# A transformer layer on one core: attention's inverse sums as diagonal matrices in the turning products, the second tile turned by halves, the last output pieces signalled singly

## The reference, cut to what matters

```python
def dsa_attention(q, k, v, qi, ki, wi, k_sel):       # 8 heads of 64, queries in 2 blocks of 128
    ...
        logits = jnp.einsum('bqhd,bqkhd->bhqk', qb, ks) * (HEAD_DIM ** -0.5)
        logits = jnp.where(ok[:, None], logits, -jnp.inf)
        p = jax.nn.softmax(logits, axis=-1)
        return jnp.einsum('bhqk,bqkhd->bqhd', p, vs)

def peer_ffn(h, peer_wq, sub_keys1, sub_keys2, peer_u, peer_v):
    q = (h @ peer_wq).reshape(B, T, PEER_HEADS, PEER_QDIM)
    q1, q2 = q[..., :PEER_HALF], q[..., PEER_HALF:]
    s1 = jnp.einsum('bthd,nd->bthn', q1, sub_keys1)
    s2 = jnp.einsum('bthd,nd->bthn', q2, sub_keys2)
    ...                                               # top 16 of each, top 16 of the sums, softmax: gates
    a = gelu(einsum('td,tkd->tk', h, peer_u[eid]));  out = einsum('tk,tkd->td', gate * a, peer_v[eid])

h = h + concat([attention, pooling]) @ w_out
h = h + peer_ffn(rms_norm(h), ...)
return h[:, N_META:]
```

## Time and profile before

| what | value |
|---|---|
| runs | 988.92, 990.38, 988.08 us; median 988.92 |
| span of the profiled execution | 986.2 us, granted TensorE clock 1.000 |
| PE busy | 965.7 us (98%), 6472 records |
| DVE, ACT, POOL busy | 683.2, 465.5, 192.2 us |
| 2 costliest PE lines | L1796 369.3 us, L1444 321.5 us and 64.3 us |

### The profile page before, as it was taken

How to read it: one execution, slowest core, us unless ns; L and a number is a source line. 1 busy time by engine, 2 the same in 40 slices (tenths; PEclk the granted TensorE clock), 3 DMA queues, 4 the chain that set the end, 5 groups by cost and what they waited for, 6 DMA issues and landing times.

```text
span 986.2 us, 18565 instructions
## 1 busy us (share of the span) xinstructions
PE 965.7 (98%) x6472; PEld 885.2 (90%) x6472; DVE 683.2 (69%) x1275; ACT 465.5 (47%) x718; POOL 192.2 (19%) x234
## 2 busy tenths in 40 slices
PE   7999999899999999999999999999999999999998
PEld 7998899888999788999999999999999999999997
DVE  5899758898988786656666565666656565666655
ACT  5566545533777434444344444434344444434442
POOL 3064227986877000000000000000000000000000
PEclk9999999999999999999999999999999999999999
DMA  8634139745212676454555555455555545455554
GB/s 245 187 124 131 46 90 335 190 116 149 79 55 84 217 240 222 172 207 175 194 189 184 199 174 207 172 198 185 185 198 176 207 171 202 180 191 192 178 205 149
DMA packets 70164, 172.57 MB, mean 175 GB/s; under 512 B 6752, under 2 KB 35552, under 8 KB 69616
## 3 DMA queue, kind: packets, MB, share of 16 engines
q1 hardware_dynamic: 68080, 167.47, 50.0%
q0 software_dynamic: 576, 4.19, 2.1%
q10 hardware_dynamic: 1472, 0.44, 0.2%
HBM read 163.16 MB, written 4.72 MB: 170 GB/s over the span
## 4 chain that ended last, share of the span: by engine, by line
PE 74%; DVE 1%; issue 0%; ACT 0%; DVEq 0%; POOL 0%
PE psum L1796 35%; PE psum L1444 31%; PE psum L1754 6%; PE psum L1761 2%; PE psum L1685 1%; DVE big L1111 0%; DVE rr L1207 0%; DVE big L1237 0%; ACT rr L754 0%; ACT big L705 0%; DVE big L1122 0%; PE psum L1742 0%; DVEq L102 0%; ACT raw L700 0%; ACT rr L739 0%
## 5 line engine op out<-in xcount | busy, mean ns | idle before, releaser
L1796 PE MATMUL psum<-rr 128*128 128x512 f32 x1536 | 369.3, 391 | 1.1 <-issue 0.7
L1796 PEld LDWEIGHTS psum<-rr 128*128 128x128 f32 x1536 | 280.7, 188 | 56.2 <-issue 0.9
L1444 PEld LDWEIGHTS psum<-h_all,rr 128*128 128x128 f32 x2592 | 318.8, 188 | 8.3
L1444 PE MATMUL psum<-h_all,rr 128*128 128x256 f32 x2592 | 321.5, 280 | 0.0
L1177 DVE TENSOR_TENSOR rr<-raw,rr 128x1024 fp32r<-128x1024 f32 x109 | 133.5, 1225 | 216.4 <-ACT rr L748 216.4
L748 ACT ACTIVATE rr<-raw 128x1024 fp32r<-128x1024 f32 x109 | 115.6, 1061 | 293.6 <-PE psum L1796 293.6
L633 ACT ACTIVATE rr<-raw 128x1024 fp32r<-128x1024 f32 x107 | 113.6, 1061 | 48.1 <-DMA raw<-in_peer_u_dram 48.1
L1116 DVE TENSOR_TENSOR rr<-raw,rr 128x1024 fp32r<-128x1024 f32 x108 | 131.7, 1219 | 0.5 <-ACT rr L633 0.2
L1163 DVE TENSOR_TENSOR rr<-psum,picks 128x2048 fp32r<-128x2048 f32 x32 | 72.4, 2288 | 9.4 <-PE psum L1754 7.7
L1444 PE MATMUL psum<-rr,h_all 128*128 128x256 f32 (+1 forms) x528 | 64.3, 282 | 0.4 <-POOL rr L1254 0.3
L1754 PE MATMUL psum<-raw,rr 128*128 128x128 f32 x512 | 63.2, 277 | 0.8 <-issue 0.6
(11 more groups left out here) (199 smaller groups left out, 826.2 us busy)
## 6 DMA issues: line engine op xcount, KB each, us to landing
raw<-in_peer_u_dram SPq DMA_DIRECT2D x128, 512.0 KB, 4.1
raw<-in_peer_v_dram SPq DMA_DIRECT2D x128, 512.0 KB, 3.5
big<-in_w_in_dram SPq DMA_DIRECT2D x10, 1024.0 KB, 5.9
big<-in_peer_wq_dram SPq DMA_DIRECT2D x8, 1024.0 KB, 5.9
big<-in_w_out_dram SPq DMA_DIRECT2D x4, 1024.0 KB, 5.2
rr<-big POOLq DMA_DIRECT2D x4, 1024.0 KB, 8.2
up_kept<-gel SPq DMA_DIRECT2D x20, 128.0 KB, 3.7
gel<-up_kept SPq DMA_DIRECT2D x20, 128.0 KB, 3.6
```

Source lines behind the costliest of these rows:

```text
L1444: i = pe.matmul(dst, lhs(a, k), rhs(b, k), start=(n == 0), stop=(n == 3 * DK - 1))
L1796: i = pe.matmul(psum[:, 4 + 2 * t + n, :], g_sp[:, s, x, t * P:(t + 1) * P], v_sp[s][:, y, n * 512:(n + 1) * 512], start=(first and m == 0 ...
```

## The change

1. `probs` becomes `inverse_diagonals`. DVE no longer multiplies the exponentials. It takes the reciprocals and writes for each head a 128x128 diagonal matrix of them (`ident` times a per-partition scalar, 16 in all, into `inv_diag`, a reused part of `big`). For tile 1 the second half of the heads goes in two groups of two.
2. PE's transpositions of the exponentials become true float32 products, exponentials as weights, diagonal as moving operand: same shapes, same number (40). Each waits for its own head's diagonal.
3. Tile 1 is turned by halves: meta and first 128 keys of heads 0 to 3, then meta of heads 4 to 7 (which raises `pe_pt` to 3), then the first 128 keys of heads 4 to 7 (`pe_pt` 4).
4. The sub-keys are transposed on the host and loaded straight into `kt_sub`. `ksub`, PE's two transpositions and ACT's copy go.
5. `o_done` rises after each of the first three output pieces, and DVE waits for each singly.

```diff
-        ksub = take(2 * P).rearrange("p (a n) -> p a n", a=2)
+        inv_diag = big[:, z_at + 2048:z_at + 2048 + 12 * P].rearrange("p (h n) -> p h n", h=12)
+        def diag_slot(t, h):
+            return h if t == 0 else NH + h if h < NH // 2 else h - NH // 2
...
-            sp.dma_start(ksub[:, 0, :], sk1[0]).then_inc(ld_g2, 16)
-            sp.dma_start(ksub[:, 1, :], sk2[0]).then_inc(ld_g2, 16)
+            sp.dma_start(kt_sub[:, 0, :], sk1[0]).then_inc(ld_g2, 16)
+            sp.dma_start(kt_sub[:, 1, :], sk2[0]).then_inc(ld_g2, 16)
...
-            act.wait_ge(pe_ks, 1)
-            act.activation(kt_sub, psum[:, 6, 0:2 * P].rearrange("p (a n) -> p a n", a=2), ACT.Copy).then_inc(ks_ev, 1)
...
-            def probs(t, h0, h1):
-                k = KEYS[t]
-                lg = rel[:, NH * KOFF[t]:NH * (KOFF[t] + k)].rearrange("p (h k) -> p h k", h=NH)
+            def inverse_diagonals(t, h0, h1):
                 dve.wait_ge(a_exp, NH * t + h1)
                 of, to = (slice(n + 8 * t + h0, n + 8 * t + h1) for n in (144, 160))
                 dve.reciprocal(stat[:, to], stat[:, of]).then_inc(d_seq, 1)
                 dve.wait_ge(d_seq, seq.up())
-                dve.tensor_tensor(lg[:, h0:h1], lg[:, h0:h1], stat[:, to].unsqueeze(2).to_broadcast([P, h1 - h0, k]), ALU.mult)\
-                   .then_inc(d_prob, 1)
+                for h in range(h0, h1):
+                    dve.tensor_scalar(inv_diag[:, diag_slot(t, h), :], ident, stat[:, 160 + 8 * t + h:161 + 8 * t + h], None, ALU.mult)\
+                       .then_inc(d_prob, 1)
...
-            probs(1, 0, NH // 2)
-            probs(1, NH // 2, NH)
+            inverse_diagonals(1, 0, NH // 2)
+            for h in range(NH // 2, NH, 2):
+                inverse_diagonals(1, h, h + 2)
...
             for t in range(2):
-                if t == 0:
-                    dve.wait_ge(o_done, 1)
-                else:
-                    dve.wait_ge(c_done, NK)
                 for n in range(2):
+                    if t + n < 2:
+                        dve.wait_ge(o_done, 2 * t + n + 1)
+                    else:
+                        dve.wait_ge(c_done, NK)
                     a = t * D + n * 512
                     dve.tensor_tensor(big[:, a:a + 512], raw[:, a:a + 512], psum[:, 4 + 2 * t + n, :], ALU.add).then_inc(d_out, 1)
...
-            def turn_probs(t, r, first, b, halves=(2, 2)):
-                for h in range(NH):
-                    if h % 4 == 0:
-                        pe.wait_ge(d_prob, halves[h // 4])
+            def turn_probs(t, r, first, b, heads):
+                for h in heads:
+                    pe.wait_ge(d_prob, NH * t + h + 1)
                     a = NH * KOFF[t] + h * KEYS[t] + first
-                    i = pe.transpose(psum[0:r, b + h // 4, (h % 4) * P:(h % 4 + 1) * P], rel[:, a:a + r], ident)
-                i.then_inc(pe_pt, 1)
+                    i = pe.matmul(psum[0:r, b + h // 4, (h % 4) * P:(h % 4 + 1) * P], rel[:, a:a + r], inv_diag[:, diag_slot(t, h), :],
+                                  start=True, stop=True)
+                return i
...
+                heads = range(4 * half, 4 * half + 4)
+                turn_probs(0, P, META, 2, heads)
+                pe.wait_ge(z_ev, z_after(N_IN - 1))
+                turn_probs(0, META, 0, 0, heads).then_inc(pe_pt, 1)
             attend(0, ((1, 0), (0, 2)))
-            turn_probs(1, META, 0, 0, (3, 4))
-            turn_probs(1, P, META, 2, (3, 4))
+            turn_probs(1, META, 0, 0, range(NH // 2))
+            turn_probs(1, P, META, 2, range(NH // 2))
+            turn_probs(1, META, 0, 0, range(NH // 2, NH)).then_inc(pe_pt, 1)
+            turn_probs(1, P, META, 2, range(NH // 2, NH)).then_inc(pe_pt, 1)
             pe.wait_ge(pt_ev, 3)
-            turn_probs(1, P, META + P, 0, (3, 4))
+            turn_probs(1, P, META + P, 0, range(NH)).then_inc(pe_pt, 1)
...
-            pe.wait_ge(ld_g2, 32)
-            for a in range(2):
-                i = pe.transpose(psum[:, 6, a * P:(a + 1) * P], ksub[:, a, :], ident)
-            i.then_inc(pe_ks, 1)
...
-            pe.wait_ge(ks_ev, 1)
+            pe.wait_ge(ld_g2, 32)
...
-                    if last and t == 0 and n == 1:
-                        i.then_inc(o_done, 1)
+                        if last and t + n < 2:
+                            i.then_inc(o_done, 1)
...
+    if name in ("sub_keys1", "sub_keys2"):
+        return a.transpose(0, 2, 1)
```

More of the change, by code:

```diff
@@ L243, in layer @@
         a_soft, b_ev, ut_hi, v_hi, a_gel = sem("a_soft"), sem("b_ev"), sem("ut_hi"), sem("v_hi"), sem("a_gel")
-        ks_ev, pk_ev, ohg_up, zt_ev = sem("ks_ev"), sem("pk_ev"), sem("ohg_up"), sem("zt_ev")
+        pk_ev, ohg_up, zt_ev = sem("pk_ev"), sem("ohg_up"), sem("zt_ev")
         d_ms, d_t32, d_lo, w_lo_e, d_seq = sem("d_ms"), sem("d_t32"), sem("d_lo"), sem("w_lo_e"), sem("d_seq")
@@ L269, in layer @@
         pe_x, z_done, pe_ix, pe_sc, pe_y = sem("pe_x"), sem("z_done"), sem("pe_ix"), sem("pe_sc"), sem("pe_y")
-        pe_qk, pe_log, pe_pt, pe_cat, pe_ks = sem("pe_qk"), sem("pe_log"), sem("pe_pt"), sem("pe_cat"), sem("pe_ks")
+        pe_qk, pe_log, pe_pt, pe_cat = sem("pe_qk"), sem("pe_log"), sem("pe_pt"), sem("pe_cat")
         pe_zt = sem("pe_zt")
@@ L998, in cat_low @@
                        .then_inc(cat_lo, 1)
-            probs(0, 0, NH // 2)
-            probs(0, NH // 2, NH)
+            inverse_diagonals(0, 0, NH // 2)
+            inverse_diagonals(0, NH // 2, NH)
             def keep_half(half):
@@ L1595, in _ @@
             for half in range(2):
-                pe.wait_ge(d_prob, half + 1)
-                for r, first, b in ((P, META, 2), (META, 0, 0)):
-                    if b == 0:
-                        pe.wait_ge(z_ev, z_after(N_IN - 1))
-                    for h in range(4 * half, 4 * half + 4):
-                        a = h * KEYS[0] + first
-                        i = pe.transpose(psum[0:r, b + half, (h % 4) * P:(h % 4 + 1) * P], rel[:, a:a + r], ident)
-                i.then_inc(pe_pt, 1)
+                heads = range(4 * half, 4 * half + 4)
+                turn_probs(0, P, META, 2, heads)
+                pe.wait_ge(z_ev, z_after(N_IN - 1))
+                turn_probs(0, META, 0, 0, heads).then_inc(pe_pt, 1)
             attend(0, ((1, 0), (0, 2)))
-            turn_probs(1, META, 0, 0, (3, 4))
-            turn_probs(1, P, META, 2, (3, 4))
+            turn_probs(1, META, 0, 0, range(NH // 2))
+            turn_probs(1, P, META, 2, range(NH // 2))
+            turn_probs(1, META, 0, 0, range(NH // 2, NH)).then_inc(pe_pt, 1)
+            turn_probs(1, P, META, 2, range(NH // 2, NH)).then_inc(pe_pt, 1)
             pe.wait_ge(pt_ev, 3)
-            turn_probs(1, P, META + P, 0, (3, 4))
+            turn_probs(1, P, META + P, 0, range(NH)).then_inc(pe_pt, 1)
             pe.wait_ge(pt_ev, 4)
```

## The result

The changed kernel is slower: median 995.2 us against 989.96 us of the kernel before (12 runs each), a ratio of 1.005 with a 95% interval of 1.0037 to 1.0064, so +3.7 to +6.3 us. The forecast was 990.3 us and "no change", with a range of 988.1 to 992.6 us; the time lies outside it.

A forecast was written before the change was run, and what follows sets the result against it. PE, busy 98% of the span, was taken as the bound. Attention +2.25, sub-keys -0.22 and the end -0.60 us gave +1.43 us on 988.92: 990.3 us, "no change", range 988.1 to 992.6 us.

The forecast's parts named there:

- Behind attention PE waits little, so I carry a shift at 113.87 us on to the end: After attention, from `w_out`'s first load: the +2.25 us shift was carried unchanged to the end of the kernel.
- full price: Rival, attention's products: each worth four transpositions, or weight loads stop prefetching at single waits; 998 us, chance 0.03.
- The 16-key chunks get no discount, since they too stream 128 moving columns: Attention's meta chunks: their products were priced like the others, 0.111 us a record and 0.222 us a product.
- The slip of ACT's exponentials: Tile 1 on ACT: exponentials of heads 4 to 7 queue behind the later meta copy and slip by 0.85 us.
- turning by halves: Tile 1: only 4 products stand behind the signal for ACT's meta copy, leaving PE a wait of 0.41 us.
- The sub-keys and the end: Two transpositions leave PE, -0.22 us; singly signalled output pieces let DVE's last additions start earlier, -0.60 us.
- swallowed later: Rival, routing: DMA transfers keep their times, so PE's 3.4 us of waits shrink by the delay; 988.1 us, chance 0.10.
- they should move along: Routing, against the swallowed delay: weight-chunk transfers hang on PE's earlier products and DVE's searches, so they shift with PE.
- slow pace: Rival, attention: 72 records on the path at 0.126 us each, +1.1 us; with single waits up to 992.6 us, chance 0.22.
- single waits: Attention: forty waits already met, taken at 0, with up to 0.03 us each, 1.2 us, as the bound.
- the missing wait for L986: Attention: PE's 0.26 + 1.76 us of waiting for DVE's two wide multiplications go entirely.
- the fourth addition: Kernel's end: DVE's last addition starts at 982.2 instead of 982.81 us, within 0.1 us of PE's end.

The follow-up runs named there:

- e5: The changed kernel with the 16 meta-chunk products using 128 weight columns, so no width changes in attention; ratio 1.0047 to the kernel before, attention 19.68 us.
- e6: The changed kernel with narrow products grouped: tile 0's second half starts with meta, tile 1 turns all meta chunks first; ratio 1.0046 to the kernel before.
- e3: The kernel before with only item 5, the first three output pieces signalled singly; ratio 0.9989 to the kernel before.
- e4: The kernel before, DVE multiplying as before, but the 40 transpositions of the exponentials are float32 products with the identity; ratio 1.0056 to the kernel before.
- e1: The kernel before with only items 1 to 3, the attention part of the change; ratio 1.007 to the kernel before.
- e15: The kernel before with 12 unused float32 products (5.2 us) on PE between attention and `w_out`; ratio 1.008 to the kernel before.
- e11: The changed kernel with half of an early up product moved ahead of the routing's wait for the fifth query chunk; ratio 1.0047 to the kernel before.
- e7: The kernel before with 8 unused float32 products (3.4 us) on PE between attention and `w_out`; ratio 1.0054 to the kernel before.

## Why the prediction was wrong, point by point

**The bound.** Right: PE at 98%, and the expert blocks are the same before and after (743.1 us from the picks to PE's end in both). Wrong was the sentence "Behind attention PE waits little, so I carry a shift at 113.87 us on to the end": behind the shift the routing grew by 2.9 us in the profile.

**The price of a product.** 0.112 us a record, as said. The "full price" rival is refuted: 32 records, 16 products, in 3.67 us in e5, 0.224 us for a product. The Trainium skill (TensorE: Matmul & The Clock Gate, section Terms) gives the transpose mode as 4 times faster for FP32; this trace does not agree, it shows twice.

**Attention, +2.25 forecast, +3.31 measured.** The step that failed is "The 16-key chunks get no discount, since they too stream 128 moving columns". They pay extra, when their width differs from the neighbour's: for float32 products a pair of changes costs 0.3 us, and there are four pairs. For transpositions the same change costs nothing visible: 12 loads, 8 narrow and 4 wide, take 1.19 us, and 12 loads, 4 narrow and 8 wide, 1.24 us. The first of these is the row that I read as the price of a width; only 8 of its loads are narrow, and all are transpositions. Without width changes (e5) attention is 19.68 us, and the forecast was 116.12 - 96.58 = 19.54 us. The Trainium skill (TensorEngine Tiling (Array Packing), section Restrictions) says that column tiling rules out the transpose mode for FP32. That would fit products of 16 columns being run as tiles and transpositions not; that this switch is what costs 0.3 us is my reading, and no run here shows it.

**DVE, ACT, the waits.** The diagonals were in time, the last at 105.1 us, for a product at about 107.4 us (both with the later start). The slip of ACT's exponentials was right in kind: its last one ended at 103.7 us, where the weight copy behind it starts,

```profile
103.70 1.89 ACT L452 ACTIVATE rr<-big 128x2048 fp32r<-128x2048 f32 x1
```

against 101.99 us before, 1.7 us later (0.85 forecast, and 0.35 from the start; the other 0.5 fits the three width changes ahead of that signal). The diagonals of heads 0 to 3 took 1.89 us instead of 0.88:

```profile
102.00 1.89 DVE L986 TENSOR_SCALAR big<-cst,big 128x128 f32<-128x128 f32 x4
```

That cost nothing: they were done at 103.9 us, and PE took the first at 104.7 us and the last at 105.4 us. What doubled their time is not shown. The wait for ACT's copy that "turning by halves" leaves was there, 0.40 us in e5, and the old order hides it (e6).

**The sub-keys and the end.** -0.22 and -0.60 forecast. PE's first routing scores stand 32.67 us after `w_out`'s start, 32.88 before; the end is shorter by 0.8 us after the change and by 0.6 us in e3, and the fourth addition starts 0.05 us behind PE's end. Both right in size.

**The routing, 0 forecast, +2.9 measured in the profile.** This is the second step that failed, and the larger one: the routing stood in the sum at nothing. The rival "swallowed later" had the right place and the wrong sign. Of "they should move along", POOL's issues did: counted from `w_out`'s first load, the first three came 0.2 to 0.3 us later than before. The landings did not (9.8 and 7.9 us after the issue before, 8.3 and 8.4 us after), PE's waits grew by 1.6 us, and the clock's fall took 1.4 us. The prediction weighed no fall of the clock because the one profile had none. That a shift makes long waits and falls more frequent is what the runs show; why the DMAs land when they do, and when a wait costs the clock, stays open.

**The absolute time.** The runs with a reported span lie 1.8 us above it, not 2.7. So the profiled execution took about 988.0 us, and was one of the quicker ones of a kernel whose median is 989.96 us by the longer series. Its routing of 125.2 us at full clock is the good case, which its own program does not always meet (129.8 us in e3). Of the 4.9 us between the forecast of 990.3 us and the 995.2 us measured, 1.0 is this base, 1.1 the attention, and the remaining 2.8 us agree with the routing's 2.9 us.

**The chances.** "Slower" had 0.31, of which 0.22 for a slow pace. It came out slower, but neither by 0.126 us a record nor by single waits. Of the signs, the 80 records at 0.11 us, the missing wait for L986 and the fourth addition were as said; `w_out`'s start at 117.53 us lies just past the bound of 117.5 us, and the routing's DMA waits grew to 5.0 us where they should have stayed near 3.4.

## What to carry to other kernels

Where PE is the bound, moving a multiplication from DVE into a transposition doubles that transposition's price on PE (0.11 to 0.22 us), so it pays only if more waiting than that goes; here 4.4 us of products replaced about 2.5 us of waits, and e4 shows that the waits would have gone by PE's lateness alone. Group float32 products by weight width, or pad the narrow ones. Before calling a shift neutral, look for waits of 1 us and more behind it that hang on DMAs, and for the spread of the clock over several executions, since one profile may show the lucky case.

## What the runs showed of the hardware

- Float32 products that change between 128 and 16 weight columns lose 0.3 us for each pair of changes; transpositions of the same shapes lose nothing that can be seen (e4, e5, rows 3).
- 40 single waits on semaphores that had been raised cost nothing visible at 0.112 us a record (e5).
- In nine of 18 profiles the TensorE clock was at 1.2 GHz for 3.4 us in the routing, or twice that in e1 and e15, at a cost of 1.4 us for 3.4 us. PE had waited for a DMA for 1.76 us (e11), 2.80 us (e6), or 3.0 to 5.1 us (the others), and the fall began between 0.9 us before PE resumed (e1) and 1.6 us after (e11). After waits of 2.84 us (e4) and 3.08 us (e7) it did not fall.
- The same accumulating DMA of 1 MB landed 7.9 us after its issue in the kernel before and 10.8 us in e3, two kernels that are equal up to that point.
